# Cached values two turns earlier, the last weight unit by token halves, and softmax scores as two stacked reduced-precision passes

## What is computed

```
x = x + 0.5 * swiglu(rmsnorm(x, norm_ffn1), ffn1_w_in, ffn1_w_out)      # d_ff 2816
p = rmsnorm(x, norm_mix) @ w_in_mix                                     # 1024 -> 3592 columns
x = x + concat(headnorm(hgrn2(...)) * silu(a_g), headnorm(attend(q, k, v, logf))) @ w_out
x = x + 0.5 * swiglu(rmsnorm(x, norm_ffn2), ffn2_w_in, ffn2_w_out)
y = rmsnorm(x, norm_final)

# prompt: causal softmax attention, 8 heads of 64, blocks of 128 queries, 512 keys
s = einsum('bqhd,bkhd->bhqk', qi, kf) + ci[..., None] - cum[:, :, None, :]
# new tokens: the same against 2048 cached keys and values in 16 pages of 128, and the 4 new ones
s_past = einsum('bqhd,bkhd->bhqk', qf, k_past) + cq[..., None] + suffix[:, :, None, :]
o = einsum(softmax(s)[past], v_past) + einsum(softmax(s)[new], v)
```

## Time and profile before

| | |
|---|---|
| median of 3 runs | 1293.64 us (1292.74 to 1295.45) |
| the profiled execution, own time | 1294.23 us |
| its span in the profile | 1292.3 us |
| granted TensorE clock, mean | 0.994 |
| TensorE, VectorE, ScalarE, GpSimd busy | 98%, 46%, 37%, 9% of the span |
| mixing stage | about 589 to 834 us |
| last weight product ends | 1277.9 us |

### The profile page before, as it was taken

How to read it: one execution, slowest core, us unless ns; L and a number is a source line. 1 busy time by engine, 2 the same in 40 slices (tenths; PEclk the granted TensorE clock), 3 DMA queues, 4 the chain that set the end, 5 groups by cost and what they waited for, 6 DMA issues and landing times.

```text
span 1292.3 us, 29960 instructions
## 1 busy us (share of the span) xinstructions
PE 1261.5 (98%) x12437; PEld 1180.6 (91%) x12437; DVE 589.4 (46%) x1096; ACT 474.8 (37%) x765; POOL 110.4 (9%) x247
## 2 busy tenths in 40 slices
PE   9999999999999999998898999999999999999997
PEld 8999999999999999996555666699999999999997
DVE  6644332244354433236765676645443521343433
ACT  6543221122233112434867777543222310222222
POOL 1000000000013000000223522122000000000000
PEclk9999999999999999999989999999999999999999
DMA  8323422232322352355699999333323322323301
GB/s 202 98 82 81 144 85 65 65 95 67 122 90 66 117 144 65 115 177 163 239 370 324 342 343 360 133 99 84 98 79 114 103 77 65 96 66 105 112 11 70
DMA packets 186649, 172.35 MB, mean 133 GB/s; under 512 B 11393, under 2 KB 149154, under 8 KB 186562
## 3 DMA queue, kind: packets, MB, share of 16 engines
q1 hardware_dynamic: 185394, 167.47, 41.2%
q0 software_dynamic: 1104, 3.67, 0.8%
q10 hardware_dynamic: 64, 0.02, 0.0%
HBM read 162.19 MB, written 8.93 MB: 132 GB/s over the span
## 4 chain that ended last, share of the span: by engine, by line
PE 91%; DVE 4%; issue 2%; ACT 2%; DMA 1%; SPq 0%; ACTq 0%; DVEq 0%
PE ps L2156 78%; PE ps L989 2%; PE ps L1074 2%; PE ps L1089 2%; PE ps L914 1%; DMA d_keys<-in_cache_k 1%; PE ps L954 1%; PE ps L934 1%; ACT d_keysT L1334 1%; PE ps L752 0%; PE ps L2296 0%; DMA gain_rows<-in_norm_final 0%; PE ps L895 0%; PE ps L2310 0%; DVE ps L1791 0%
## 5 line engine op out<-in xcount | busy, mean ns | idle before, releaser
L2156 PE MATMUL ps<-n_hi,w_hi 128*128 128x272 f32 x1856 | 387.1, 288 | 2.0 <-DVE w_lo L2626 0.8
L2156 PE MATMUL ps<-n_hi,w_lo 128*128 128x272 f32 x1856 | 386.8, 288 | 0.0
L2156 PE MATMUL ps<-n_lo,w_hi 128*128 128x272 f32 x1856 | 385.2, 288 | 0.0
L2346 ACT ACTIVATE w_hi<-w_raw 128x2048 fp32r<-128x2048 f32 (+2 forms) x76 | 156.0, 2052 | 540.7 <-PE ps L2156 540.6
L2156 PEld LDWEIGHTS ps<-n_hi,w_hi 128*128 128x128 f32 x1856 | 292.9, 188 | 2.7 <-issue 2.5
L2156 PEld LDWEIGHTS ps<-n_lo,w_hi 128*128 128x128 f32 x1856 | 292.7, 189 | 0.0
L2156 PEld LDWEIGHTS ps<-n_hi,w_lo 128*128 128x128 f32 x1856 | 290.7, 189 | 0.0
L2500 DVE TENSOR_TENSOR w_lo<-w_raw,w_hi 128x2048 fp32r<-128x2048 f32 (+2 forms) x75 | 191.6, 2555 | 49.5 <-ACT w_hi L2346 49.5
L2156 PE MATMUL ps<-g_hi,w_lo 128*128 128x272 f32 x704 | 145.7, 288 | 0.0
L2156 PE MATMUL ps<-g_hi,w_hi 128*128 128x272 f32 x704 | 145.5, 288 | 0.0
L2156 PE MATMUL ps<-g_lo,w_hi 128*128 128x272 f32 x704 | 145.2, 288 | 0.0
(11 more groups left out here) (360 smaller groups left out, 1230.4 us busy)
## 6 DMA issues: line engine op xcount, KB each, us to landing
w_raw<-in_ffn_w_in SPq DMA_DIRECT2D x87, 512.0 KB, 4.9
d_keys<-in_cache_k SPq DMA_DIRECT2D x128, 256.0 KB, 5.3
d_values<-in_cache_v SPq DMA_DIRECT2D x124, 256.0 KB, 6.1
w_raw<-in_w_in_mix SPq DMA_DIRECT2D x28, 512.0 KB, 4.7
w_raw<-in_ffn_w_out SPq DMA_DIRECT2D x16, 768.0 KB, 5.5
w_raw<-in_ffn_w_out SPq DMA_DIRECT2D x16, 640.0 KB, 4.8
w_raw<-in_w_out_mix SPq DMA_DIRECT2D x8, 512.0 KB, 4.9
suffix_scratch<-d_log_f_sums SPq DMA_DIRECT2D x32, 64.0 KB, 2.1
```

Source lines behind the costliest of these rows:

```text
L2156: mm = pe.matmul(bank(4 * j + 2 * t + half), wp, xp[:, k, half * HALF:(half + 1) * HALF], start=(k == 0 and wp is w[0] and xp is x_hi), st ...
L2346: nc.scalar.activation(w_hi[j][:, 0:kt * UC], w_raw[j][:, 0:kt * UC], ACT.Copy).then_inc(w_hi_ready, 1)
```

## The change

- *Values.* `value_turn` is two turns earlier: 8b + 7 + k for half 0 and 8b + 11 + k for half 1; for the last sequence 8b + 7 + k and 8b + 11 + k // 2. The assignment of partitions stays. The first pair of a half now stands behind both halves of the scores. The copies of the outputs, the transposes of the probabilities for half 0 (turn 8b + 6 instead of 8b + 7) and their combination over groups (turn i = 3 instead of 4) move with it.
- *Softmax scores.* The f32 matmul becomes two F32R matmuls of 128 rows. The first multiplies the rounded queries, stacked twice, by the rounded keys and their remainders (`q_one`, `k_one`); the second the remainder of the queries by the rounded keys, and in its other 64 rows the picking rows by the gate sums, split in upper and lower part (`q_two`, `k_two`). VectorE gets a subtraction and a scaled subtraction for each head, ScalarE a second copy, GpSimd the zeroing by multiplication instead of memset, the picking rows and one or two copies of the keys. For the first two heads GpSimd does this in turns 41 and 43 instead of 38 and 39; the parts that depend on a finished copy stand one turn later (`stage_turn(h) + 1`).
- *Tail.* The last unit of FFN2 runs its 544 tokens as two halves of 272, each over both feature tiles. Additions, squares and sums follow by quarters; the norm factors of the first two token tiles are made before those of the other three. Of 40 transposes 8 stand before the last column sums and 32 behind; the last store is one DMA for the whole row of 1024, so nine in all.
- The small norm tiles of the recurrent heads move to a place of their own.

```diff
         def value_turn(b, half, k):
             if b == DB - 1:
-                return 8 * b + (9 if half == 0 else 11) + k // 2
-            return 8 * b + (9 if half == 0 else 13) + k
+                return 8 * b + (7 + k if half == 0 else 11 + k // 2)
+            return 8 * b + (7 if half == 0 else 11) + k
...
+        def stage_turn(h):
+            return (FOX_AT - 2, FOX_AT)[h] if h < 2 else unit_at(3 * (h - 2) + 2) + 1
...
         def fox_scores_tensor(pe, x):
...
                 for t in UNIT_TILES[r]:
-                    pe.matmul(ps[:, B_L, c0:c0 + (t + 1) * P], q_aug[j][:, t * P:(t + 1) * P], k_aug[j][:, 0:(t + 1) * P],
-                              start=True, stop=True, skip_group_check=True).then_inc(fs_done, 1)
+                    out, q, k = ps[:, B_L, c0:c0 + (t + 1) * P], slice(t * P, (t + 1) * P), slice(0, (t + 1) * P)
+                    pe.matmul(out, q_one[j][:, q], k_one[j][:, k], start=True, stop=False, skip_group_check=True)
+                    pe.matmul(out, q_two[j][:, q], k_two[j][:, k], start=False, stop=True, skip_group_check=True)\
+                        .then_inc(fs_done, 1)
...
-            if i == 7 and b < DB:
+            if i == 6 and b < DB:
                 pe.wait_ge(dexp[0], 2 * b + 2)
...
-            for w, (b, half, k) in values_of(x):
-                values(w, b, half, k)
+            due = values_of(x)
+            late = any(k == 0 for _, (b, half, k) in due)
+            if not late:
+                for w, (b, half, k) in due:
+                    values(w, b, half, k)
             if active:
                 scores(y, 1)
+            if late:
+                for w, (b, half, k) in due:
+                    values(w, b, half, k)
...
         def fox_stage_vector(dve, x):
...
+                    nc.vector.tensor_copy(k_one[j][half, :], k).then_inc(k_staged, 1)
+                    dve.wait_ge(k_staged, 3 * h + 1)
+                    nc.vector.tensor_tensor(k_one[j][other, :], k, k_one[j][half, :].bitcast(F32), ALU.subtract)\
                         .then_inc(k_staged, 1)
+                if x == stage_turn(h) + 1:
+                    dve.wait_ge(q_staged, 2 * h + 2)
+                    nc.vector.scalar_tensor_tensor(q_two[j][0:DH, :], pT[half, T_FQ + h // 2, 0:SEQ], SCALE,
+                                                   q_one[j][half, :].bitcast(F32), ALU.mult, ALU.subtract).then_inc(k_staged, 1)
...
+            def last_unit(pair, kt, x_hi, x_lo):
...
+                for half in range(2):
+                    for t in range(2):
+                        if (half, t) == (1, 1):
+                            pe.wait_ge(sq_summed, TAIL_SUM + 2)
+                            column_sums(ps[:, 4, :], range(2))
+                        for k in range(kt):
+                            mm = products(1, kt, t, k, (half,), x_hi, x_lo)
+                        mm.then_inc(mm_done, 1)
...
             pe.wait_ge(drained, units - 1)
-            for i in range(3):
-                if i == 2:
-                    pe.wait_ge(drained, units)
-                transposes(i, 0, range(4)).then_inc(yt_done[0], 1)
-                transposes(i, 1, range(4, 6))
-            pe.wait_ge(sumsq_ready, 4)
...
+            pe.wait_ge(xg_ready, 8)
+            tile_transposes(0)
+            pe.wait_ge(sq_summed, TAIL_SUM + 4)
+            column_sums(ps[:, 6, :], range(2, TT + 1))
+            tile_transposes(1)
```

261 lines of the change are left out of this document (175 added, 86 removed).

## The result

The changed kernel takes 1301.53 us (median of 5, 1300.60 to 1302.29) against 1293.64 us (1292.42 to 1295.45): a ratio of 1.0058, 95% interval 1.0044 to 1.0072, so 7.6 us slower. Its profiled execution has a span of 1299.8 us where the one before had 1292.3.

A forecast was written before the change was run, and what follows sets the result against it. It took TensorE to bound the mixing stage, with DMA engines full: 17.3 - 1.7 - 5.6 + 1.5 + 1.5 - 3.3 = +9.7 us, so 1303 us by the median; range 1287 to 1310, likeliest case 1297 to 1309.

The forecast's parts named there:

- The clash: Mixing stage: values and scores want the same columns in 30 turns, 0.86 us each, 25.8 us in all, 17.3 paid.
- The factor of 0.85: Turns 44 to 64 and the softmax scores: share of added or saved TensorE time taken as paid or gained.
- The 12.67 us of the earlier trace: A wait for a key transfer amid turns 15, 16, 19 and 20, said to absorb most clashes there: 1.0 us paid.
- rival 1: Mixing stage: clash real but mostly hidden by slack in the transfers; 10.3 us instead of 17.3, about 1296; chance 0.15.
- The value term as a whole: Values two turns earlier: +17.3 us for clashes, -1.7 for the last sequence, +1.5 for probabilities one turn earlier.
- The probabilities one turn earlier: TensorE's transposes for half 0 in turn 8b+6 wait for exponentials in four early turns: +1.5 us (0 to 5).
- The scores: Softmax heads: reduced passes gain 0.83 us a head, 6.6 for eight, -5.6 us at 0.85 paid.
- The GpSimd queue: Staging from turn 41, 7 to 12.3 us ahead of turn 43's group maxima: just in time, 0, up to +6 us.
- rival 3: Every clash paid, VectorE's additions paid twice over, GpSimd late, scores gain little: +24 us, 1317; 0.16 for all over 1309.
- The casts: GpSimd's four casts in the staging at turn 41: 0.6 us each as copies, 1.5 if like a multiplication.
- VectorE's additions: Staging of the heads: a subtraction and a scaled subtraction a head on VectorE cost +1.5 us, between 0 and 8.
- The end: From last weight product to span end: 14.4 us falls to 10.8 to 12.5; -3.3 us (-1.4 to -4.2).

The follow-up runs named there:

- The values alone: The kernel before with only the value schedule (value turns, copies, transposes and combination moved): 1304.68 us, ratio 1.0078.
- the free columns: The changed kernel, cached scores of clashing turns from 11 on written to partition groups the values don't use (outputs wrong): 1290.51 us, ratio 0.9974.
- the doubled dose: The kernel before with value products moved onto the scores' partition groups, so all 56 turns with one value pair clash: 1320.19 us, ratio 1.0197.
- one pass: The kernel before with one reduced-precision score pass a tile, no added staging: 1295.16 us, 1.0003; the same on the values' new turns: 1298.32 us, 1.0031.
- The padding: The kernel before with five more 64x512 multiplications by zero on GpSimd in turns 41 and 43 each, small norm tiles moved: 1300.76 us, ratio 1.0051.
- the scores alone: The kernel before with only the stacked softmax scores and their staging: 1298.90 us, ratio 1.0035.
- the memsets: GpSimd's zeroing of 64 spare rows by memset instead of multiplication: changed kernel 1300.02 us, 1.0037; kernel before with only the stacked scores 1297.32 us, 1.0024.
- using the maxima later: The changed kernel with VectorE's and ScalarE's use of the group maxima back in turn i = 4 instead of 3: 1303.04 us, ratio 1.0063.
- VectorE padded: The kernel before with two more 64x512 operations a head on VectorE, into unused rows: 1295.64 us, ratio 1.0009.
- the tail alone: The kernel before with only the tail part of the change: 1290.75 us, ratio 0.9970.

## Why the prediction was right, step by step

The forecast was 1303 us, the measured time is 1301.5; the sum of +9.7 us stands against +7.6. The term of the values was 7 us too high and that of the scores 5 us or more too low, so the number is better than its parts: two errors of opposite sign nearly cancelled, and that was luck. (By itself the score part came out 8.6 us above its terms of -5.6 and +1.5, within the whole 5.5.)

- **The clash: right in kind and in size of one, over-counted in what is paid.** A clash costs 0.86 us of TensorE (0.89 to 1.75), as worked out from the two blocks of 0.99 us and the lone pairs. The Trainium skill (TensorE: Matmul & The Clock Gate, Part 3, Measured speedup vs the span model) gave an estimate of 0.64 us for it; the blocks of this case do not agree with that, two value and score passes side by side cost no more than the scores alone. Of the 25.8 us I called 17.3 paid. The values alone show 12.5 us by turn 63: 6.3 us for the 18 clashes ahead of turn 43 (I had 9.3 for 19), and 6.2 us for the ten from there on (I had 8.0 for eleven); these have the other costs of the new turns in them, and the free columns give 11 us for 28 clashes, 0.39 us each. The factor of 0.85 was read from the share of TensorE's lines in the chain; the doubled dose gives 0.67 / 0.86 = 0.78 behind turn 43 and 0.40 ahead of it. Part of what absorbed the rest is seen: TensorE's 3.7 us of waits for keys are gone in all kernels with slower value blocks. The 12.67 us of the earlier trace rows were a transfer's piece of the chain; TensorE stood still for only 3.1 us around it, so less could be absorbed there than I read from it. This is the slack of rival 1, which had 10.3 us for the term; the measured 11 us lie between the two and close to the rival's.
- **The value term as a whole:** 17.3 - 1.7 + 1.5 = 17.1 us predicted, 10.1 measured. At the end 1.7 us come back (from +12.7 at turn 63 to +11.0 at the stage's end), with the values alone 1.2. The probabilities one turn earlier were given 1.5 us; the free columns leave the stage 0.5 us shorter than before with all of that in place, so they cost little, or the shorter scores pay for them.
- **The scores: the passes right, their worth wrong.** I had 0.83 us a head; the units fall by 6.2 / 8 = 0.78, or 0.71 over the first seven heads, whose units hold no wait. But "at 0.85 paid" failed: without other changes 10 us of saved TensorE time are worth nothing, with the values' new turns 6 us. The step that failed took a high share in the chain of waits for a price of saved time. The share says that TensorE's work is in line; it does not say that the next limit is far. The DMA engines stood at 0.99, and with one pass transfers enter the chain; how much of the lost 10 us they hold is open, since 3.5 us of it is a hole without a releaser.
- **The GpSimd queue: foreseen and mis-sized.** I counted 7 us of staging and 3.1 us of maxima from 725.5 and found it just in time, 0 in the sum and up to +6. The staging took 7.9 us and the maxima 3.6, so they were 1.5 us late. The padding shows that such a queue by itself makes 6.6 us, and with the scores alone head 1's 7.1 us ahead of the group sums, which I left out of the count, make the jump. In the changed kernel they do not: its sums come behind head 1's staging without anyone waiting for them, and its jump of 4.6 us is 1.6 us of clashes, a wait for exponentials of 2.4 us and 3.6 us at half clock, less what the shorter scores give. Of all that, the memsets gave back 1.5 to 2.7 us, and using the maxima later nothing. Two terms were missing from the sum: VectorE's work of both changes in one turn, and the clock behind a hole. As for rival 3, its queue came true in part and the rest of it did not; its terms as listed also add up to +27, not +24.
- **The casts** cost 0.61 to 0.95 us, for 8 rows of 512 as for 64, near the lower of my two bounds; the multiplications 1.5 us for 64 rows as for 8.
- **VectorE's additions:** 1.5 predicted, 1.2 measured in the kernel before, where they stand by themselves. The Trainium skill (SBUF — State Buffer, SBUF: two separate sides) would have GpSimd take turns with VectorE's two-input operations; in the kernel with VectorE padded that is not to be seen, GpSimd's copies of 8x512 take 606 ns on average as they did without them (605). In the changed kernel it agrees: from 700 us on VectorE's subtraction of 64x512 (L1751) takes 0.69 us when nothing runs on GpSimd and 0.98 four times of eight, each time beside a GpSimd operation, and GpSimd's cast of 64x512 (L2080) 0.61 to 0.97. It is a few tenths at a time.
- **The end:** 3.3 predicted, 3.9 and 3.3 measured (by the ratio and by the medians), from 14.7 to 10.4 us behind the last product and 0.5 us more inside the last unit. That TensorE would keep its clock was right. The idle time was misread: ahead of the column sums it was 0.9 us, with 0.2 us before that, and not 1.8, and it is 0.7 us now, not under 0.5.

That scores and values together cost less than apart would fit one picture: the clashes slow TensorE below its transfers, and then shorter scores count. That shorter scores are worth more with the new turns is shown for the one-pass scores (0 and 6 us); the reason, and that it explains the 3.1 us between the sum of the parts and the whole, are argued.

Of all kernels measured with whole outputs the one with the tail alone is the best, 1290.75 us (0.9970, 0.9959 to 0.9981).

## What to carry to other kernels

Where two matmul streams of 32-row tiles share a block, write down for each turn which columns each one writes; a schedule that moves one stream by half a period can turn a free product into a full-price one, and no wait in the profile will name it. Ask of saved time on the busiest engine what limits next (here the DMA engines stood at 0.99) before giving it a price. Before more work goes into a lightly loaded queue, look for the small steps in it that others wait for: 7.8 us of dead work on GpSimd in front of 3 us of group sums cost 6.6 us. When two changes are joined, list what each puts on every engine in the same turn: here either alone left TensorE a wait of 0.2 or 0.6 us, both together 2.4. And look at the granted clock behind every new hole; part of the price stands there and not in the wait. Before a wait is put down to a change, see whether it lies where the change can act, and whether it is as long in a kernel that leaves that stage alone.

## What the runs showed of the hardware that was not expected

- Value products on other columns than the scores next to them are free, 0.89 to 1.00 us for the block with or without them; on the same columns the block is exactly the sum, 1.75 to 1.85 us.
- GpSimd takes the same time for 8 rows of 512 as for 64: 0.61 us a cast, 1.5 us a multiplication by a scalar. A memset of 64x512 takes 0.52 us.
- Behind a hole of 3.1 to 3.8 us on TensorE the granted clock was 0.50 for some 7 us, behind one of 2.4 us for 3.6 us; behind one of 2.1 us in the kernel with the maxima used later it stayed at 1.00, so the length of the hole alone does not decide it.
- With the DMA engines at 1.00, TensorE stood still for 3.5 us once with no releaser in the profile.
